# A layer's shift and scale: the products on GpSimd in place of TensorE's row products

## The chip, the cores and the metric

The kernel runs on one core of a Trainium2 chip. The metric is the device time of one launch in microseconds, the median of the runs. The profile is one further execution of the same program.

## The reference, cut to what matters

Two layers work on x of 256 tokens by 1024 channels, all in float32. Each layer is a token mixer (gated linear attention in the first, block attention, "MoBA", in the second) and an MLP. Ahead of each of these four parts x is normalised and then shifted and scaled by vectors that come from one conditioning vector c:

```python
c_act = jax.nn.silu(c)
for i in range(DEPTH):                       # 2
    mod = (c_act @ ada_w[i] + ada_b[i])      # ada_w[i]: 1024 x 6144
    sh1, sc1, g1, sh2, sc2, g2 = jnp.split(mod, 6, axis=-1)
    h = rms_norm(x, norm_mix_g[i]) * (1 + sc1) + sh1
    x = x + g1 * mixer(h)
    h = rms_norm(x, norm_mlp_g[i]) * (1 + sc2) + sh2
    x = x + g2 * (jnp.square(jax.nn.relu(h @ w1[i])) @ w2[i])
```

The product c_act @ ada_w is cut into 24 blocks of 512 columns, 12 a layer; a block's weights are 1024 x 512 numbers, 2 MB. Blocks 18 to 21 are the shift and scale (sh2, sc2) of the last MLP. They are what is changed.

## The kernel before, in words

Large products run on TensorE in three passes: ScalarE rounds a unit of weights to w_hi (line 860), VectorE subtracts to get w_lo (line 1186), and TensorE adds hi x hi, lo x hi and hi x lo (lines 428 to 430). Weights come from HBM by SyncE's queue into w_raw, eight units deep; w_hi and w_lo are rings of four units. A unit is 128 x 1024 numbers. Every engine's order is written out by hand, with semaphores between them.

A block of the second mixer's input projection (`moba`, six blocks n = 0 to 5) is four units. Behind a unit TensorE may do side work, held in `sides[n][u]`; ScalarE and VectorE have such lists under `tasks`, keyed by the block whose weights they prepare. From block 1 on each block is read out of PSUM, its heads' square sums are taken, it is rotated (`cosines`, `rotate`, `scale` on VectorE), and turned by TensorE (`turn_rot`, line 768).

The modulation blocks come in three ways. Most are loaded in two halves of 1 MB (512 of the 1024 rows of weights, as 128 partitions x 4 x 512) into the two halves of `ada_raw` by GpSimd's queue. VectorE multiplies the four slices of a half by their numbers of c_act and adds them into a slot of `ada_acc` (lines 1201 and 1204), and TensorE sums over the partitions: `fin_mods` (line 471) for shift and scale, sixteen products of a 128x128 piece with a column of ones, or `fin_gate` (line 503) for the gates. Blocks 0 to 3 and blocks 18 to 21 go to TensorE directly: `ada_rows` (line 488) makes four products for a half, each with one column of c_act as the stationary side, into partitions 0, 32, 64 and 96 of one bank; ScalarE copies the rows out (`ada_out`, line 900), and `ada_cols` (line 496) turns and sums them with a selector column in four small products. For blocks 18 to 21 the eight row groups stand behind units 1 and 2 of blocks 1 to 4 of `moba`, the selector groups behind unit 1 of blocks 2 to 5, and VectorE first clears the bank (`zero_rows`, line 1301). VectorE then adds the bias and makes the scale (`mods(3, 1)`), which TensorE waits for ahead of the attention's scores.

GpSimd's queue does nothing but start loads: each when the half of `ada_raw` that it overwrites has been used. Block 18 is loaded late in the first MLP; blocks 19 to 22 are each loaded when TensorE's row products have used the half before.

Of the kernel before, what the change touches and what calls it, by code (L numbers as in the profile page):

```python
# [28 lines left out]
ALU = mybir.AluOpType  # L29
ACT = mybir.ActivationFunctionType  # L30
X_AXIS = mybir.AxisListType.X

P = 128
TB = 2
COLS = 512
# [12 lines left out]
def trunk_kernel(nc, x_d, c_d, pos_d, ada_w, ada_b, mix_g, mlp_g, gla_in, gla_up, gla_bg, gla_og,  # L48
# [22 lines left out]
    mix_w = [(gla_in[0], gla_out[0]), (moba_in[0], moba_out[0])]  # L71


    ADA_PE = [[0, 2, 1, 3], [18, 19, 20, 21]]

    ctx = ExitStack()
    with ctx:
# [3 lines left out]
        def sem(name):  # L81
            return ctx.enter_context(nc.semaphore(name))
# [5 lines left out]
        ada_raw = sb("ada_raw", [P, 2, KC // 2, COLS])  # L88
        ada_acc = sb("ada_acc", [P, ADA_ACC, COLS])
# [9 lines left out]
        rows = sb("rows", [P, P])  # L99
        cols = sb("cols", [P, P])  # L100
        c_act = sb("c_act", [P, KC])
# [10 lines left out]
        K1 = 1024  # L112
# [3 lines left out]
        def area(at, *shape):  # L116

            n = 1
            for s in shape:
                n *= s  # L120
            assert at + n <= ARENA
            v = arena[:, at:at + n]
            if len(shape) == 2:
                v = v.rearrange("p (a b) -> p a b", a=shape[0])
            elif len(shape) == 3:
                v = v.rearrange("p (a b c) -> p a b c", a=shape[0], b=shape[1])
            return v
# [41 lines left out]

        ada_pre = [area((4 + 2 * i) * K1, KC // 2, COLS) for i in range(4)]  # L170

        ada_row = [area(13 * K1, 2, COLS)[0:97], area(10 * K1, 2, COLS)[0:97]]

        ps = ctx.enter_context(nc.psum_tensor("ps", [P, 8, COLS], F32))

# [13 lines left out]
        ada_mac = sem("ada_mac")  # L189
        set_up = sem("set_up")  # L190
        ada_sw_in = [sem(f"ada_sw_in{i}") for i in range(2)]
        ada_pre_in = [sem(f"ada_pre_in{i}") for i in range(4)]
        ada_pe = sem("ada_pe")
        row_ok = sem("row_ok")
        col_T = sem("col_T")
        c_in, c_T, c_ok = sem("c_in"), sem("c_T"), sem("c_ok")
        vec_T, vec_ok = sem("vec_T"), sem("vec_ok")
        mod_T, mod_red, mod_ok = sem("mod_T"), sem("mod_red"), sem("mod_ok")
        gate_p, gate_ok = sem("gate_p"), sem("gate_ok")
# [30 lines left out]

        ADA_FIRST = ADA_PE[0]
        SETS_SILU_SIN, SETS_LN_EXP = "silu_and_others", "natural_log_exp_and_others"

        def ada_turn(b):

            return b - 8 if isinstance(b, int) and b > ADA_PE[1][-1] else b - 4

# [7 lines left out]
        def acc_slot(b):  # L249
            return (b + 4) % ADA_ACC  # L250
# [25 lines left out]
        @block.gpsimd  # L276
        def _(pool):
            for half in range(2):
                pool.wait_ge(ada_pe, 6 + half + 1)
                nc.gpsimd.dma_start(ada_raw[:, half], ada_part(4, half)).then_inc(ada_sw_in[half], 16)  # L280

            def load(l, n, half):
                src = ada_w[l, half * 4 * P:(half + 1) * 4 * P, bass.ds(n * COLS, COLS)]
                nc.gpsimd.dma_start(ada_raw[:, half], src.rearrange("(k p) n -> p k n", p=P)  # L284
                                    ).then_inc(ada_sw_in[half], 16)


            for l, first, end in ((0, 5, 12), (1, 0, 7)):
                with pool.Fori(first, end) as n:
                    for half in range(2):  # L290
                        pool.wait_ge(ada_mac, 8 * n + 8 * ada_turn(12 * l - 1) + 4 * (half + 1))
                        load(l, n, half)
            with pool.Fori(7, 11) as n:
                for half in range(2):
                    pool.wait_ge(ada_pe, 2 * n - 2 * 7 + 8 + half + 1)
                    load(1, n, half)
            for half in range(2):
                pool.wait_ge(ada_mac, 8 * ada_turn(22) + 4 * (half + 1))
                load(1, 11, half)
# [124 lines left out]
        def _(pe):  # L424
# [40 lines left out]
            def fin_mods(v, bank):  # L465

                b0 = 12 * (v // 2) + 6 * (v % 2)
                pe.wait_ge(ada_mac, 8 * (ada_turn(b0 + 3) + 1))
                for i in range(4):
                    for q in range(4):  # L470
                        z = mm(ps[:, bank, 4 * i + q:4 * i + q + 1],
                               ada_acc[:, acc_slot(b0 + i), q * P:(q + 1) * P], ones[:, 0:1], start=True, stop=True)
                z.then_inc(mod_T, 1)

            def ada_rows(b, half, bank):


                if b in (0, 3):
                    raw = ada_raw[:, half]
                    pe.wait_ge(ada_in[half], 16 if b == 0 else 32)  # L480
                elif b < 4:
                    raw = ada_pre[2 * (2 - b) + half]
                    pe.wait_ge(ada_pre_in[2 * (2 - b) + half], 16)
                else:
                    raw = ada_raw[:, half]
                    pe.wait_ge(ada_sw_in[half], 16 * (b - 3))
                for k in range(4):
                    z = mm(ps[32 * k:32 * k + 1, bank, :], c_act[:, 4 * half + k:4 * half + k + 1], raw[:, k],  # L488
                           start=half == 0, stop=half == 1)
                z.then_inc(ada_pe, 1)  # L490

            def ada_cols(i, bank, c0=0):

                pe.wait_ge(row_ok, i + 1)
                for q in range(4):
                    z = mm(ps[:, bank, c0 + q:c0 + q + 1], ada_row[i // 4][:, i % 2, q * P:(q + 1) * P],  # L496
                           ones[0:97, 0:1], start=True, stop=True)
                z.then_inc(col_T, 1)

# [245 lines left out]
            def moba():  # L745
# [2 lines left out]
                    for i in range(2):  # L748
                        fin_gate(16 + i, 2 + i)

                def rows(i, half):

                    if i == 0:
                        pe.wait_ge(set_up, 3)
                    elif half == 0:
                        ada_cols(3 + i, 1, 4 * (i - 1))
                    ada_rows(18 + i, half, 0)

                def turn_rot(n):

                    pe.wait_ge(rot_ok, n + 1)
# [36 lines left out]
                        z.then_inc(oT_ok, 1)  # L798

                sides = [{}, {0: gate1}] + [{3: (lambda n=n: turn_rot(n))} for n in range(4)]  # L800
                for i in range(4):
                    for half in range(2):
                        sides[1 + i][1 + half] = lambda i=i, half=half: rows(i, half)
                sides[5][1] = lambda: ada_cols(7, 1, 12)
                for n in range(6):
                    if n >= 2:
                        pe.wait_ge(in_out, 12 + 2 * (n - 1))
# [36 lines left out]
        def _(act):  # L844
# [51 lines left out]
            def ada_out(i):  # L896
                act.wait_ge(ada_pe, 2 * i + 2)
                if i >= 2:
                    act.wait_ge(col_T, i - 1)
                A(ada_row[i // 4][:, i % 2], ps[0:97, 6 + i % 2 if i < 4 else 0, :], ACT.Copy).then_inc(row_ok, 1)  # L900

            def modulate_tile(v, tb, quarters):

# [119 lines left out]
            def moba():  # L1023
# [29 lines left out]
                def read_v(half):  # L1053
                    read_in(1, 4 + half, [b_v[:, tb, half * COLS:(half + 1) * COLS] for tb in range(TB)])

                tasks = {}
                for n in range(4):
                    tasks.setdefault((n + 2, 3), []).append(lambda n=n: ada_out(4 + n))
                    tasks.setdefault((n + 1, 3), []).append(lambda n=n: stats(n))
                    tasks.setdefault((n + 3 if n < 3 else 6, 3 if n == 3 else 0), []).append(lambda n=n: read_rot(n))  # L1060
                tasks[5, 3] = [lambda: read_v(0), lambda: ada_out(7)]
                tasks[(6, 3)] = [lambda: read_v(1), lambda: read_rot(3)]

                tasks[1, 0] = [sines]
# [108 lines left out]
        def _(dve):  # L1173
# [46 lines left out]
            def mods(v, bank):  # L1220

                l, s = v // 2, v % 2
                if v == 3:
                    dve.wait_ge(col_T, 8)
                else:
                    dve.wait_ge(mod_T, v)
                at = C_AB + (4 * l + 2 * s) * KC
                V.tensor_tensor(modc[:, l, 2 * s:2 * s + 2].rearrange("p a k -> p (a k)"), ps[:, bank, 0:2 * KC],
                                cols[:, at:at + 2 * KC], ALU.add).then_inc(mod_red, 1)
                dve.wait_ge(mod_red, 4 + v)  # L1230
                g = (C_MLP if s else C_MIX) + l * KC
                m = modc[:, l, 2 * s + 1]
                V.scalar_tensor_tensor(m, m, 1.0, cols[:, g:g + KC], op0=ALU.add, op1=ALU.mult
                                       ).then_inc(mod_ok, 1)
# [47 lines left out]
            def first_norm():  # L1282
# [11 lines left out]
                for i in range(2, 4):  # L1294
                    first_mods(i, ADA_FIRST[i], 4 + i)
                modulate(0, slice(0, SEQ), 0, 0, range(2, 4))

            def zero_rows():

                dve.wait_ge(a_ok, A_NORM[2] + 8)  # L1300
                V.memset(ps[:, 0, :], 0.0).then_inc(set_up, 1)

            def norm(v):

# [355 lines left out]
            for l in range(DEPTH):  # L1660
                if l == 0:
                    gla()
                else:
                    norm(2)
                    zero_rows()
                    moba()
                out_project(l)
                norm(2 * l + 1)
                mlp(l)
# [39 lines left out]
```

## Time and profile before

| | us |
|---|---|
| median of 3 runs | 687.27 |
| lowest and highest | 686.78, 690.5 |
| profiled execution, span from first to last instruction | 686.4 |
| TensorE busy | 646.6 |
| VectorE busy | 470.6 |
| ScalarE busy | 338.4 |
| GpSimd busy (starting DMAs) | 30.3 |

Of the profiled execution the page gives the span and no other time; the median is 0.9 us above it. The engines are called PE (TensorE; PEld its weight loads), DVE (VectorE), ACT (ScalarE), POOL (GpSimd) and SP (SyncE). L428 is line 428 of the kernel before. Matmuls are pipelined, so the spacing of their starts says more than their durations.

### The profile page before, as it was taken

The numbers are of one execution on the slowest core, as the hardware profiler recorded it, in microseconds if no ns is written. First come the engines' busy times: TensorE is split into PE (matmuls) and PEld (weight loads), VectorE is DVE, ScalarE is ACT, GpSimd is POOL, SyncE is SP. The second block draws the span as 40 slices with busy tenths as digits, with TensorE's granted clock in tenths as the row PEclk, the third lists the DMA queues.
The fourth block names the chain that finished last, engine by engine and source line by source line (L and its number), as shares of the span: only waits on it lengthen the run. The fifth ranks groups of instructions, "written<-read, shape, count | busy, mean of one in ns | idle before, by whom it ended". The sixth has DMA issues, their size and how long they took to land.

```text
span 686.4 us, 9712 instructions
## 1 busy us (share of the span) xinstructions
PE 646.6 (94%) x3594; PEld 535.0 (78%) x3594; DVE 470.6 (69%) x702; ACT 338.4 (49%) x562; POOL 30.3 (4%) x44
## 2 busy tenths in 40 slices
PE   4789999999999999999997999989999999999997
PEld 2457866677789988998885666667779998999885
DVE  2358999696787877787886846685678844555446
ACT  3244632544854345435427756665585445443440
POOL 0011010000000000000000000000000000000000
PEclk9889999999999999999999999999999999999999
DMA  8999778554598877878935677760349555565501
GB/s 305 380 377 352 244 265 309 198 176 154 181 317 311 296 250 270 317 258 287 343 118 183 221 270 246 259 230 1 123 145 336 193 185 187 184 182 198 195 32 61
DMA packets 61492, 156.87 MB, mean 229 GB/s; under 512 B 4124, under 2 KB 5000, under 8 KB 61464
## 3 DMA queue, kind: packets, MB, share of 16 engines
q1 hardware_dynamic: 50584, 114.56, 48.3%
q0 software_dynamic: 10880, 41.95, 17.5%
q8 instruction: 17, 0.28, 0.2%
q14 instruction: 11, 0.09, 0.0%
HBM read 155.44 MB, written 1.05 MB: 228 GB/s over the span
## 4 chain that ended last, share of the span: by engine, by line
PE 77%; DVE 12%; ACT 6%; DMA 2%; issue 2%; SPq 1%; ACTq 0%; DVEq 0%; POOLq 0%
PE ps L428 16%; PE ps L429 15%; PE ps L430 15%; PE ps L582 8%; PE ps L581 8%; PE ps L580 8%; DVE w_lo L1186 3%; ACT w_hi L860 2%; PE ps L488 2%; DVE ada_acc L1204 1%; DMA rows<-in_ada_b_dram 1%; DMA ada_raw<-in_ada_w_dram 1%; DVE a_lo L1329 1%; PE ps L512 1%; PE ps L496 1%
## 5 line engine op out<-in xcount | busy, mean ns | idle before, releaser
L1186 DVE TENSOR_TENSOR w_lo<-w_raw,w_hi 128x1024 fp32r<-128x1024 f32 x192 | 232.4, 1222 | 140.7 <-ACT w_hi L860 140.5
L860 ACT ACTIVATE w_hi<-w_raw 128x1024 fp32r<-128x1024 f32 x192 | 200.4, 1057 | 222.7 <-PE ps L430 116.8
L428 PE MATMUL ps<-w_hi,a_hi 128*128 128x512 f32 x288 | 121.1, 421 | 20.1 <-DVE a_lo L1329 14.1
L580 PE MATMUL ps<-a_hi,w_hi 128*128 128x256 f32 x448 | 126.9, 283 | 0.0
L582 PE MATMUL ps<-a_hi,w_lo 128*128 128x256 f32 x448 | 126.8, 283 | 0.0
L581 PE MATMUL ps<-a_lo,w_hi 128*128 128x256 f32 x448 | 126.8, 283 | 0.0
L429 PE MATMUL ps<-w_lo,a_hi 128*128 128x512 f32 x288 | 116.0, 403 | 0.0
L430 PE MATMUL ps<-w_hi,a_lo 128*128 128x512 f32 x288 | 115.5, 401 | 0.0
L428 PE MATMUL ps<-w_hi,m_hi 128*128 128x512 f32 x256 | 100.7, 393 | 0.0
L429 PE MATMUL ps<-w_lo,m_hi 128*128 128x512 f32 x256 | 100.4, 392 | 0.0
L430 PE MATMUL ps<-w_hi,m_lo 128*128 128x512 f32 x256 | 100.3, 392 | 0.0
L428 PEld LDWEIGHTS ps<-w_hi,a_hi 128*128 128x128 f32 x288 | 56.2, 195 | 47.2 <-issue 16.9
L1204 DVE SCALAR_TENSOR_TENSOR ada_acc<-ada_raw,c_act,ada_acc 128x512 f32<-128x512 f32 (+1 forms) x112 | 84.0, 750 | 3.5
L581 PEld LDWEIGHTS ps<-a_lo,w_hi 128*128 128x128 f32 x448 | 85.9, 192 | 0.6
L580 PEld LDWEIGHTS ps<-a_hi,w_hi 128*128 128x128 f32 x448 | 85.9, 192 | 0.5
L582 PEld LDWEIGHTS ps<-a_hi,w_lo 128*128 128x128 f32 x448 | 85.9, 192 | 0.0
L430 PEld LDWEIGHTS ps<-w_hi,a_lo 128*128 128x128 f32 x288 | 56.2, 195 | 12.5
L429 PEld LDWEIGHTS ps<-w_lo,a_hi 128*128 128x128 f32 x288 | 56.3, 196 | 10.6 <-issue 0.2
L428 PEld LDWEIGHTS ps<-w_hi,m_hi 128*128 128x128 f32 x256 | 48.5, 190 | 11.2 <-issue 1.4
L430 PEld LDWEIGHTS ps<-w_hi,m_lo 128*128 128x128 f32 x256 | 48.5, 189 | 10.2
L429 PEld LDWEIGHTS ps<-w_lo,m_hi 128*128 128x128 f32 x256 | 48.5, 189 | 9.6
L284 POOL DMA_DIRECT2D ada_raw<-in_ada_w_dram x38 | 28.5, 749 | 452.5 <-DVE ada_acc L1204 359.0
(158 smaller groups left out, 509.1 us busy)
## 6 DMA issues: line engine op xcount, KB each, us to landing
w_raw<-in_mlp_w_dram SPq DMA_DIRECT2D x64, 1024.0 KB, 5.4
ada_raw<-in_ada_w_dram POOLq DMA_DIRECT2D x40, 1024.0 KB, 6.0
w_raw<-in_gla_w_in_dram SPq DMA_DIRECT2D x12, 1024.0 KB, 11.1
w_raw<-in_moba_w_in_dram SPq DMA_DIRECT2D x12, 1024.0 KB, 6.3
ada_raw<-in_ada_w_dram SPq DMA_DIRECT2D x4, 1024.0 KB, 10.8
arena<-in_ada_w_dram SPq DMA_DIRECT2D x4, 1024.0 KB, 12.8
w_raw<-in_gla_w_out_dram SPq DMA_DIRECT2D x4, 1024.0 KB, 7.7
w_raw<-in_moba_w_out_dram SPq DMA_DIRECT2D x4, 1024.0 KB, 5.1
```

Source lines behind the costliest of these rows:

```text
L284: nc.gpsimd.dma_start(ada_raw[:, half], src.rearrange("(k p) n -> p k n", p=P)).then_inc(ada_sw_in[half], 16)
L428: mm(out, hi, w_hi[:, slot, wc], start=first, stop=False)
L429: mm(out, hi, w_lo[:, slot, wc], start=False, stop=False)
L430: return mm(out, lo, w_hi[:, slot, wc], start=False, stop=last)
L488: z = mm(ps[32 * k:32 * k + 1, bank, :], c_act[:, 4 * half + k:4 * half + k + 1], raw[:, k], start=half == 0, stop=half == 1)
L496: z = mm(ps[:, bank, c0 + q:c0 + q + 1], ada_row[i // 4][:, i % 2, q * P:(q + 1) * P], ones[0:97, 0:1], start=True, stop=True)
L580: mm(o, w_hi[:, u, w], a_hi[:, a, :], start=u == 0 and k == 0, stop=False)
L581: mm(o, w_hi[:, u, w], a_lo[:, a, :], start=False, stop=False)
L582: z = mm(o, w_lo[:, u, w], a_hi[:, a, :], start=False, stop=u == 3 and k == 1)
L860: A(w_hi[:, c % SPLIT], w_raw[:, c // 2, c % 2], ACT.Copy).then_inc(hi_made, 1)
L1186: V.tensor_tensor(w_lo[:, c % SPLIT], w_raw[:, c // 2, c % 2], w_hi[:, c % SPLIT].bitcast(F32), ALU.subtract).then_inc(lo_made, 1)
L1204: z = V.scalar_tensor_tensor(acc, w, s, acc, op0=ALU.mult, op1=ALU.add)
```

## The change

Blocks 18 to 21 are multiplied and summed by GpSimd, in place, in `ada_raw`: a half (128 x 2048 numbers) is multiplied by c_act, spread over the 512 columns; its four slices are then added to two, and these to one, which goes into a slot of `ada_acc` (the second half with one more sum). A wait on a semaphore stands between each two instructions. The first write into a slot waits until TensorE has read the block that the slot held before. After each half GpSimd starts the next load into it. TensorE's eight row groups and four selector groups for these blocks go, with VectorE's clearing of the bank and ScalarE's four copies; behind unit 1 of block 5 TensorE does `fin_mods(3, 1)`, which waits for GpSimd's last sum.

```diff
-            with pool.Fori(7, 11) as n:
+            pool.wait_ge(c_ok, 1)
+            for t, b in enumerate(ADA_POOL):          # 18, 19, 20, 21
+                acc = ada_acc[:, acc_slot(b)]
                 for half in range(2):
-                    pool.wait_ge(ada_pe, 2 * n - 2 * 7 + 8 + half + 1)
-                    load(1, n, half)
+                    i = 2 * t + half
+                    w = ada_raw[:, half]
+                    pool.wait_ge(ada_sw_in[half], 16 * (b - 3))
+                    nc.gpsimd.tensor_tensor(w, w, c_act[:, 4 * half:4 * half + 4, None].to_broadcast([P, 4, COLS]),
+                                            ALU.mult).then_inc(pool_mul, 1)
+                    pool.wait_ge(pool_mul, i + 1)
+                    nc.gpsimd.tensor_tensor(w[:, 0:2], w[:, 0:2], w[:, 2:4], ALU.add).then_inc(pool_sum, 1)
+                    pool.wait_ge(pool_sum, 3 * t + 1 + half)
+                    if i == 0:
+                        pool.wait_ge(gate_p, 4)
+                    elif i == 4:
+                        pool.wait_ge(mod_T, 2)
+                    if half == 0:
+                        nc.gpsimd.tensor_tensor(acc, w[:, 0], w[:, 1], ALU.add).then_inc(pool_ada, 1)
+                    else:
+                        nc.gpsimd.tensor_tensor(w[:, 0], w[:, 0], w[:, 1], ALU.add).then_inc(pool_sum, 1)
+                        pool.wait_ge(pool_sum, 3 * t + 3)
+                        pool.wait_ge(pool_ada, i)
+                        nc.gpsimd.tensor_tensor(acc, acc, w[:, 0], ALU.add).then_inc(pool_ada, 1)
+                    pool.wait_ge(pool_ada, i + 1)
+                    load(1, b + 1 - 12, half)
...
             def fin_mods(v, bank):
-                pe.wait_ge(ada_mac, 8 * (ada_turn(b0 + 3) + 1))
+                if v == 3:
+                    pe.wait_ge(pool_ada, 2 * len(ADA_POOL))
+                else:
+                    pe.wait_ge(ada_mac, 8 * (ada_turn(b0 + 3) + 1))
...
-                for i in range(4):
-                    for half in range(2):
-                        sides[1 + i][1 + half] = lambda i=i, half=half: rows(i, half)
-                sides[5][1] = lambda: ada_cols(7, 1, 12)
+                sides[5][1] = lambda: fin_mods(3, 1)
...
-                    tasks.setdefault((n + 2, 3), []).append(lambda n=n: ada_out(4 + n))
...
-                tasks[5, 3] = [lambda: read_v(0), lambda: ada_out(7)]
+                tasks[5, 3] = [lambda: read_v(0)]
...
-                    zero_rows()
```

## Rows read from the trace of the kernel before

**Rows 1.** The page: engines' busy time, and the chain's shares.
```profile
PE 646.6 (94%) x3594; PEld 535.0 (78%) x3594; DVE 470.6 (69%) x702; ACT 338.4 (49%) x562; POOL 30.3 (4%) x44
PE 77%; DVE 12%; ACT 6%; DMA 2%; issue 2%; SPq 1%; ACTq 0%; DVEq 0%; POOLq 0%
```

**Rows 2.** Timelines, 341 to 364 us: start, duration, engine, line, form [idle before].
```profile
341.29 1.88 PE L503 MATMUL ps<-ada_acc,ones 128*128 128x512 f32 x4
341.56 0.76 DVE L1560 CAST m_hi<-arena 128x512 fp32r<-128x512 f32 x2 [2.22 <-PE ps L430]
...
363.08 0.77 PE L428 MATMUL ps<-w_hi,a_hi 128*128 128x512 f32 x1 [2.79 <-DVE a_lo L1329]
```

**Rows 3.** Timeline of TensorE around the row and selector groups.
```profile
398.67 0.40 PE L430 MATMUL ps<-w_hi,a_lo 128*128 128x512 f32 x1
398.91 0.95 PE L496 MATMUL ps<-ones,arena 97*128 97x1 f32 x8
399.79 1.04 PE L488 MATMUL ps<-ada_raw,c_act 128*1 128x512 f32 x8
400.76 0.50 PE L428 MATMUL ps<-w_hi,a_hi 128*128 128x512 f32 x1
...
419.27 0.39 PE L430 MATMUL ps<-w_hi,a_lo 128*128 128x512 f32 x1
419.59 1.04 PE L488 MATMUL ps<-ada_raw,c_act 128*1 128x512 f32 x8
420.56 0.50 PE L428 MATMUL ps<-w_hi,a_hi 128*128 128x512 f32 x1
...
446.63 0.95 PE L496 MATMUL ps<-ones,arena 97*128 97x1 f32 x8
```

**Rows 4.** Timelines of TensorE and of VectorE, block 3.
```profile
411.94 0.50 PE L428 MATMUL ps<-w_hi,a_hi 128*128 128x512 f32 x1 [0.63 <-DVE w_lo L1186]
...
414.52 1.23 DVE L1186 TENSOR_TENSOR w_lo<-w_raw,w_hi 128x1024 fp32r<-128x1024 f32 x1
...
417.81 2.35 DVE L1186 TENSOR_TENSOR w_lo<-w_raw,w_hi 128x1024 fp32r<-128x1024 f32 x2
```

**Rows 5.** TensorE's timeline, and the stretch behind: busy by engine, PEclk, DMA share, GB/s.
```profile
348.37 0.39 PE L430 MATMUL ps<-w_hi,m_lo 128*128 128x512 f32 x1
348.60 3.62 PE L471 MATMUL ps<-ones,ada_acc 128*128 128x1 f32 x32
352.08 0.49 PE L428 MATMUL ps<-w_hi,m_hi 128*128 128x512 f32 x1
...
355.77 0.45 PE L428 MATMUL ps<-w_hi,m_hi 128*128 128x512 f32 x1
...
352.10:355.80 3.70, 3.70 (x12) 2.91 (x12) 3.57 (x7) 0.08 (x1) 0.00 (x0) 0.55 0.00 0
```

**Rows 6.** GpSimd's timeline and its loads' time to landing; a stretch with its DMA share.
```profile
332.43 0.75 POOL L284 DMA_DIRECT2D ada_raw<-in_ada_w_dram  x1 [6.63 <-DVE ada_acc L1204]
...
387.46 0.75 POOL L284 DMA_DIRECT2D ada_raw<-in_ada_w_dram  x1 [49.01 <-PE ps L488]
...
DMA to landing us min/median/max: 5.4/5.7/10.0
...
372.85:381.15 8.30, 8.30 (x37) 6.87 (x37) 3.17 (x6) 8.15 (x14) 0.00 (x0) 1.00 0.05 18
```

**Rows 7.** Groups by form, VectorE 338 to 448 us; ScalarE 381 to 454 us.
```profile
L1186 DVE TENSOR_TENSOR w_lo<-w_raw,w_hi 128x1024 fp32r<-128x1024 f32 x27 | 32.5, 1221 | 23.2 <-ACT w_hi L860 23.0
L1340 DVE TENSOR_TENSOR arena<-ps,gates 128x512 f32<-128x512 f32 x4 | 2.8, 688 | 0.0
L1259 DVE TENSOR_SCALAR arena<-x,stat 128x1024 f32<-128x1024 f32 x2 | 1.6, 814 | 0.1
...
L1038 ACT ACTIVATE arena<-arena 128x128 f32<-128x128 f32 x32 | 9.4, 296 | 0.3
```

**Rows 8.** Waits from 352 to 381 us: total, times, longest.
```profile
DVE a_lo L1329 <- ACT a_hi L915: 5.7, 4, 3.5
DVE stat L1255 <- ACT arena L873: 0.9, 1, 0.9
```

More of the change, by code:

```diff
@@ L71, in trunk_kernel @@
     mix_w = [(gla_in[0], gla_out[0]), (moba_in[0], moba_out[0])]
-    ADA_PE = [[0, 2, 1, 3], [18, 19, 20, 21]]
+    ADA_PE = [0, 2, 1, 3]
+    ADA_POOL = [18, 19, 20, 21]
     ctx = ExitStack()
@@ L170, in trunk_kernel @@
         ada_pre = [area((4 + 2 * i) * K1, KC // 2, COLS) for i in range(4)]
-        ada_row = [area(13 * K1, 2, COLS)[0:97], area(10 * K1, 2, COLS)[0:97]]
+        ada_row = area(13 * K1, 2, COLS)[0:97]
         ps = ctx.enter_context(nc.psum_tensor("ps", [P, 8, COLS], F32))
@@ L193, in trunk_kernel @@
         ada_pe = sem("ada_pe")
+        pool_mul, pool_sum, pool_ada = sem("pool_mul"), sem("pool_sum"), sem("pool_ada")
         row_ok = sem("row_ok")
@@ L229, in trunk_kernel @@
         N_VEC = 3 + 2 * DEPTH
-        ADA_FIRST = ADA_PE[0]
+        ADA_FIRST = ADA_PE
         SETS_SILU_SIN, SETS_LN_EXP = "silu_and_others", "natural_log_exp_and_others"
         def ada_turn(b):
-            return b - 8 if isinstance(b, int) and b > ADA_PE[1][-1] else b - 4
+            return b - 8 if isinstance(b, int) and b > ADA_POOL[-1] else b - 4
         N_PAIRS = [0, 4, 12, 20]
@@ L495, in ada_cols @@
                 for q in range(4):
-                    z = mm(ps[:, bank, c0 + q:c0 + q + 1], ada_row[i // 4][:, i % 2, q * P:(q + 1) * P],
+                    z = mm(ps[:, bank, c0 + q:c0 + q + 1], ada_row[:, i % 2, q * P:(q + 1) * P],
                            ones[0:97, 0:1], start=True, stop=True)
@@ L749, in gate1 @@
                         fin_gate(16 + i, 2 + i)
[L751 to L757, printed above, removed]
                 def turn_rot(n):
@@ L899, in ada_out @@
                     act.wait_ge(col_T, i - 1)
-                A(ada_row[i // 4][:, i % 2], ps[0:97, 6 + i % 2 if i < 4 else 0, :], ACT.Copy).then_inc(row_ok, 1)
+                A(ada_row[:, i % 2], ps[0:97, 6 + i % 2, :], ACT.Copy).then_inc(row_ok, 1)
             def modulate_tile(v, tb, quarters):
@@ L1222, in mods @@
                 l, s = v // 2, v % 2
[L1223 to L1226, printed above, removed]
+                dve.wait_ge(mod_T, v)
                 at = C_AB + (4 * l + 2 * s) * KC
@@ L1296, in first_norm @@
                 modulate(0, slice(0, SEQ), 0, 0, range(2, 4))
-            def zero_rows():
-                dve.wait_ge(a_ok, A_NORM[2] + 8)
-                V.memset(ps[:, 0, :], 0.0).then_inc(set_up, 1)
             def norm(v):
```

## The prediction

> **What bounds the kernel now.** I read the page first. TensorE is busy for 94% of the span and holds 77% of the chain that ended last; VectorE holds 12% of it [rows 1]. So work taken from TensorE is worth its own length only where TensorE is the link that is late, and work that slows VectorE costs where VectorE is. The change touches two stretches with different limits, which the chain of waits and the timelines separate.
>
> From 341.6 to 376.8 us (end of the first MLP, then the norm ahead of the second layer) the chain runs through VectorE: its link starts at 341.56 with m_hi, and TensorE's first matmul of the new layer at 363.08 has waited 2.79 us for VectorE's a_lo [rows 2].
>
> From 381 to 454 us (the second mixer's input projection) the chain is TensorE's matmuls with the rows' products between them. A projection unit is 12 matmuls, one every 0.23 us. From the last one before a selector and row group (398.67) to the first one behind it (400.76) are 2.09 us, and with a row group alone 419.27 to 420.56, 1.29 us [rows 3]. VectorE comes second here: TensorE waited 0.63 us for w_lo at 411.94 [rows 4].
>
> **Taken from TensorE.** A row group costs 1.29 - 0.23 = 1.06 us, eight of them 8.5 us. A selector group is 2.09 - 0.23 - 1.06 = 0.80 us, four of them 3.2 us. Together 11.7 us, all on the chain.
>
> **Put on TensorE.** fin_mods(3, 1), sixteen products of 128x128 with one column, takes the place of the last selector group (446.63 [rows 3]). The same form after the first MLP takes from 348.37 to 352.08, less one pitch: 3.5 us. Behind it the nine matmuls up to 355.77 take 3.69 us instead of 9 x 0.23 = 2.07, at a granted clock of 0.55, which is near the lower level of 1.2 GHz [rows 5]; before them TensorE did only one-column products. I expect the same dip: 1.6 us more. Sum 5.1 us; bounds 3.5 (no dip) and 5.1. Raw gain: 11.7 - 5.1 = 6.6 us.
>
> **What is late next.** In blocks 3 and 4, w_lo of a block's third unit starts at 414.52 and takes 1.22, so it is ready at 415.74, 3.80 us behind TensorE's start of the second unit at 411.94; without the rows TensorE is there after 12 x 0.23 plus about 0.1 = 2.86 us, so it waits 0.95 us. The fourth is ready at about 418.97 (the first of the two from 417.81 [rows 4], ended 1.15 later), 7.05 behind 411.94; TensorE comes at 3.80 + 2.86 = 6.7 and waits 0.35. Two blocks at 1.3 us take 2.6 us of the gain. In block 5 the 3.5 us of fin_mods cover this wait; in blocks 1 and 2 w_lo is further ahead. Remaining gain: 6.6 - 2.6 = 4.0 us. Bounds: 2.5 if block 2 loses as much, 6 without the clock dip.
>
> **Edits at nothing.** VectorE's clearing of a bank goes (one 128x512 instruction, not on the chain). ScalarE loses four copies of 97x512; it has idle time in these blocks, so no time comes back. The eight loads of blocks 19 to 22 no longer wait for TensorE (387.46 the first) but for GpSimd's own sums, and start from about 346 us on. POOL's queue holds nothing else before block 23, which VectorE takes up only in the second MLP. The DMA engines have room there: share 0.05 from 372.85 to 381.15 [rows 6]. If that cover were gone, w_raw would land later, and it has no slack worth naming in the blocks.
>
> **Put on GpSimd: its own time.** Per half a product over 2048 elements, a sum over 1024, a sum over 512, and per block one more of 512: 28 instructions, 30720 elements a partition. The trace has no arithmetic of GpSimd. Lower bound, VectorE's rows: 1.22 us for 1024 elements and 0.69 for 512 [rows 7], so 0.53 for 512 more and 2.28 for 2048; a block is 2 x 2.28 + 2 x 1.22 + 3 x 0.69 = 9.1 us, four are 36 us. Upper bound, far off: ScalarE's 0.296 us for 128 elements, 2.3 ns each [rows 7], 71 us. I take 36, since the row nearest in kind is VectorE's same instruction. The eight DMA instructions on POOL are 0.75 each, 6 us [rows 6].
>
> The Trainium skill's GPSIMD Engine Reference, "Performance versus the Vector engine", gives 4497 ns for a tensor_tensor of 2048 fp32. No run here shows it yet; the sum would then be about 68 us, an estimate.
>
> The first half is issued at 332.43 and lands 5.7 us later, 338.1 [rows 6]. TensorE wants the sums after the second unit of block 5, at 446.6 less the 8 us it gained till there, about 438. Between are 100 us. With 36 + 6 or 71 + 6 us GpSimd is early by itself: off the chain. The wait of TensorE on pool_ada has behind it all of TensorE, but it is met. The wait on gate_p is met with TensorE's gate products of 341.29, 1.88 us long [rows 2]; the one on mod_T with the products of 348 to 352.
>
> **Put on VectorE.** This term decides. w_lo, with two inputs in SBUF, takes 1.22 us for 1024 elements, while a one-input tensor_scalar of the same size takes 0.81 [rows 7]: VectorE has a second way into SBUF, which it uses either for a second input or for speed. If GpSimd's reads go that way too, the two engines exclude each other. Nothing in the trace shows it, since GpSimd computes nothing there. Bounds: 0, and the whole of GpSimd's time. A gain is excluded, as VectorE waits for nothing that GpSimd makes.
>
> With exclusion: GpSimd does 3.5 us of its work before 341.6 and holds back nothing. The other 36 - 3.5 = 32.5 us start beside VectorE's chain. That chain has over 40 instructions with two SBUF inputs or in the fast form, more than GpSimd's 26 left, so each of GpSimd's can fall between two of them. Hidden are VectorE's own waits up to 376.8, 5.7 + 0.9 us for ScalarE [rows 8], and its instructions that read PSUM and one SBUF tensor, six of 0.69 (four residual products, two gates; [rows 7] has the product), 4.1 us. Charged: 32.5 - 10.7 = 22 us. Once TensorE waits that long its clock falls as behind 2.79 us of idling (0.77 for the first matmul at 363.08 [rows 2] against 0.5 elsewhere); I add 2 us.
>
> SBUF — State Buffer, "Who interferes with whom", says it as a rule: a VectorE instruction with two SBUF inputs, or in a two-port mode, contends with a GpSimd instruction that reads SBUF, and whichever starts second is blocked for the other's full length. The trace agrees only in that two forms of one size differ, 0.81 against 1.22 us. By the rule with the skill's price above, the charge would be near 68 - 3.5 - 10.7 = 54 us, an estimate.
>
> **Sum, forecast (exclusion, GpSimd at VectorE's pace).** -4 + 22 + 2 = +20 us on the span of 686.4, 706.4. The median of the runs, 687.27, lies 0.9 us above that span, so 707. Its own range: 697 (half of GpSimd's time slips into waits) to 720.
>
> **Rivals.**
> 1. No contention, GpSimd off the chain. For it: no instruction of VectorE's w_lo is stretched beside POOL's DMA issues (mean 1221 ns over the window [rows 7]), though those are no reads of SBUF. Against it: the 0.81 against 1.22. Time: 687.3 - 4.0 = 683.3, from 681.3 to 685. This is the other side: faster. It decides if VectorE's instructions keep their lengths from 341 to 377 us.
> 2. Exclusion with GpSimd at its upper bound: 71 - 3.5 - 10.7 = 57 us charged, +2 - 4: 742; with longer instructions somewhat more falls into waits, so 725 to 742. It speaks for it that the engine is a different one and the only bound above is far; against it that instructions of 4 to 5 us would be needed.
> 3. Contention by shares: both engines go on, VectorE's port-using instructions stretched. From 341.6 to 376.8 they are about 23 us (35.2 less 10.7 and some issue time); half as long again adds 11, less 4: 694 to 700.
> 4. GpSimd late without contention: it decides from 94 us for 30720 elements, 3.1 ns each, above both bounds. At 4 ns it ends at 338 + 123 + 6 = 467, 29 us late: 712.
>
> **How the numbers follow.** Forecast 0.34, rival 1 0.29, rival 2 0.17, rival 3 0.16, rival 4 0.04. 0.5% is 3.4 us, about what a measurement here can tell from no change: faster means below 683.8. Rival 1 gives 0.17 below and 0.12 within; 0.03 of rival 3 falls within as well. Faster 0.17, same 0.15, slower 0.68. The range 682 to 736 leaves out about 0.06 below and 0.08 above.
>
> **What would show it.** Step by step: rows products gone from 381 to 454 us, blocks 3 and 4 at 14.3 us instead of 15.9 (411.94 to the same place in the next); sixteen one-column products there with a clock near 0.5 behind them; POOL busy about 40 us from 338 on; VectorE's small instructions of 345 to 352 us and w_lo and a_lo of 358 to 376 stretched or with gaps that nothing explains, and the new layer's first matmul at about 385 instead of 363. If that matmul stays at 363 the forecast is wrong and rival 1 holds; if POOL is busy 60 us or more and the matmul comes beyond 400, rival 2.

## The result, and the profile after

The changed kernel takes 740.06 us (739.37 to 740.45, four runs) against 687.67 for the kernel before: a ratio of 1.0746, 95% interval 1.0718 to 1.0773. The profiled execution has a span of 737.7 us, 51.3 more than before. I had forecast slower, 707 us, with a range to 736; the time lies beyond it, next to rival 2 (742).

Line numbers in the rows are each kernel's own. The page's shares. TensorE's busy time has not changed [rows 1]; VectorE's has grown by 54 us and its part of the chain from 12 to 21%:

```profile
PE 646.6 (88%) x3530; PEld 538.4 (73%) x3530; DVE 524.7 (71%) x701; ACT 336.4 (46%) x558; POOL 99.1 (13%) x72
PE 64%; DVE 21%; SPq 5%; ACT 4%; DMA 3%; issue 2%; DVEq 0%; ACTq 0%; POOLq 0%
```

GpSimd's groups from 330 to 430 us (busy, mean ns of one | idle before). The product over 2048 elements takes 3.61 us, where I had put 2.28. These 28 instructions are busy for 68.1 us; in their undisturbed lengths (3.61, 2.34, 1.26) they need 62.7:

```profile
L303 POOL TENSOR_TENSOR ada_raw<-ada_raw,c_act 128x2048 f32<-128x2048 f32 x8 | 28.9, 3610 | 1.4 <-DMA ada_raw<-in_ada_w_dram 1.2
L306 POOL TENSOR_TENSOR ada_raw<-ada_raw 128x1024 f32<-128x1024 f32 x8 | 20.5, 2567 | 0.6
L315 POOL TENSOR_TENSOR ada_raw<-ada_raw 128x512 f32<-128x512 f32 x4 | 7.1, 1785 | 0.3
L318 POOL TENSOR_TENSOR ada_acc<-ada_acc,ada_raw 128x512 f32<-128x512 f32 x4 | 6.0, 1499 | 0.3
L313 POOL TENSOR_TENSOR ada_acc<-ada_raw 128x512 f32<-128x512 f32 x4 | 5.6, 1402 | 0.3
```

The two engines side by side, timelines of 348 to 366 us. Read the ends: m_lo (0.68 us before the change) starts at 348.26 and ends at 353.07, 0.56 behind the end of GpSimd's product (348.90 + 3.61 = 352.51). A tensor_scalar of 0.29 us starts at 360.96, while GpSimd starts a load, and ends at 365.43, when the product behind that load has ended (361.65 + 3.61 = 365.26). Both had started before the product that held them, by the profile 0.64 and 0.69 us (the last section comes back to this):

```profile
348.26 4.81 DVE L1570 TENSOR_TENSOR m_lo<-arena,m_hi 128x512 fp32r<-128x512 f32 x1
348.90 3.61 POOL L303 TENSOR_TENSOR ada_raw<-ada_raw,c_act 128x2048 f32<-128x2048 f32 x1
...
360.83 0.80 POOL L286 DMA_DIRECT2D ada_raw<-in_ada_w_dram  x1 [1.11 <-issue]
360.96 4.47 DVE L1639 TENSOR_SCALAR arena<-arena 128x256 f32<-128x256 f32 x1
361.65 3.61 POOL L303 TENSOR_TENSOR ada_raw<-ada_raw,c_act 128x2048 f32<-128x2048 f32 x1
```

VectorE's groups, held and not held: one of the kernel before (338 to 448 us), then the changed kernel's from 330 to 500. The forms with two SBUF inputs grow from 0.43 to 1.93 us (L1634 before, L1641 now) and from 0.69 to 2.11 (L1348); the one that reads PSUM stays at 0.68, where it had 0.69 [rows 7]:

```profile
L1634 DVE SCALAR_TENSOR_TENSOR arena<-arena 128x256 f32<-128x256 f32 x6 | 2.5, 425 | 0.2
...
L1641 DVE SCALAR_TENSOR_TENSOR arena<-arena 128x256 f32<-128x256 f32 x6 | 11.6, 1934 | 0.2
L1348 DVE TENSOR_TENSOR x<-x,arena 128x512 f32<-128x512 f32 x4 | 8.4, 2109 | 0.1
L1347 DVE TENSOR_TENSOR arena<-ps,gates 128x512 f32<-128x512 f32 x4 | 2.7, 681 | 0.0
```

And where it lands: TensorE's first matmul of the second layer, 363.08 before [rows 2], and behind it the blocks (the second unit of blocks 3 and 4, 462.62 and 477.05, is 14.43 us apart; before, 411.94 [rows 4] and 427.83, the row that stands first here, 15.89). Last, the clock behind the sixteen products of fin_mods(3), which start at 494.33:

```profile
427.83 0.50 PE L428 MATMUL ps<-w_hi,a_hi 128*128 128x512 f32 x1 [0.63 <-DVE w_lo L1186]
...
413.22 0.77 PE L452 MATMUL ps<-w_hi,a_hi 128*128 128x512 f32 x1 [11.98 <-DVE a_lo L1336]
...
462.62 0.50 PE L452 MATMUL ps<-w_hi,a_hi 128*128 128x512 f32 x1 [0.63 <-DVE w_lo L1201]
466.48 0.50 PE L452 MATMUL ps<-w_hi,a_hi 128*128 128x512 f32 x1 [0.85 <-DVE w_lo L1201]
...
477.05 0.50 PE L452 MATMUL ps<-w_hi,a_hi 128*128 128x512 f32 x1 [0.63 <-DVE w_lo L1201]
...
494.33 3.79 PE L498 MATMUL ps<-ones,ada_acc 128*128 128x1 f32 x32
...
498.00:500.70 2.70, 2.70 (x8) 2.12 (x9) 2.70 (x3) 0.00 (x0) 0.00 (x0) 0.50 0.36 51
```

VectorE's w_lo that stands behind the norm starts at 432.97 where it started at 376.80. Less 0.6 us that this execution was late already at 333 us, 55.6 us are lost between. From there to the end 4.9 us come back: 56.2 less 51.3.

Not all of the 55.6 is VectorE. The last twelve matmuls ahead of the norm's transposes start 54.47 us later than before (367.37, now 421.84, behind a wait for VectorE's a_lo), the transposes behind them 56.21 us later (370.39, now 426.60): the twelve took 3.02 us and now take 4.76, at a granted clock of 0.57, near the lower level. TensorE had waited 11.98, 1.81 and 1.01 us ahead of its three groups of matmuls from 413.22 on. So 53.9 us come from VectorE and 1.7 from TensorE's clock; the rows are two of before, two of now, and the stretch (windows, as [rows 5]):

```profile
367.37 0.47 PE L428 MATMUL ps<-w_hi,a_hi 128*128 128x512 f32 x1
370.39 1.03 PE L512 MATMUL ps<-eye,arena 128*128 128x128 f32 x8
...
421.84 0.76 PE L452 MATMUL ps<-w_hi,a_hi 128*128 128x512 f32 x1 [1.01 <-DVE a_lo L1336]
426.60 1.03 PE L539 MATMUL ps<-eye,arena 128*128 128x128 f32 x8
421.84:426.60 4.76, 4.76 (x13) 3.71 (x14) 1.32 (x2) 0.00 (x0) 0.00 (x0) 0.57 0.90 315
```

### The profile page after: what moved, and what is told of

Its sections match the earlier page's. It is cut to its first block, busy times and chain, and to the rows that moved or that the text cites. A ratio compares the mean times of both kernels' runs of the same rounds, so it can differ in the third digit from the quotient of the medians.

```text
span 737.7 us, 9577 instructions
## 1 busy us (share of the span) xinstructions
PE 646.6 (88%) x3530; PEld 538.4 (73%) x3530; DVE 524.7 (71%) x701; ACT 336.4 (46%) x558; POOL 99.1 (13%) x72
## 4 chain that ended last, share of the span: by engine, by line
PE 64%; DVE 21%; SPq 5%; ACT 4%; DMA 3%; issue 2%; DVEq 0%; ACTq 0%; POOLq 0%
PE ps L452 13%; PE ps L454 12%; PE ps L453 12%; PE ps L608 7%; PE ps L609 7%; PE ps L607 7%; DVE w_lo L1201 6%; DVE ada_acc L1219 2%; DMA w_raw<-in_gla_w_in_dram 2%; DVE arena L1641 2%; ACT w_hi L876 1%; DVE x L1348 1%; DVE a_lo L1336 1%; PE ps L498 1%; DMA ada_raw<-in_ada_w_dram 1%
## 5 line engine op out<-in xcount | busy, mean ns | idle before, releaser
L1201 DVE TENSOR_TENSOR w_lo<-w_raw,w_hi 128x1024 fp32r<-128x1024 f32 x192 | 242.7, 1276 | 138.2 <-ACT w_hi L876 138.0
L452 PE MATMUL ps<-w_hi,m_hi 128*128 128x512 f32 x256 | 102.6, 401 | 7.6 <-DVE m_lo L1570 4.7
```

The lines of the kernel that those rows point to most:

```text
L452: mm(out, hi, w_hi[:, slot, wc], start=first, stop=False)
L1201: V.tensor_tensor(w_lo[:, c % SPLIT], w_raw[:, c // 2, c % 2], w_hi[:, c % SPLIT].bitcast(F32), ALU.subtract).then_inc(lo_made, 1)
```

## The experiments

Theory: a GpSimd instruction that reads SBUF and a VectorE instruction that uses the second way exclude each other for their whole length, and GpSimd's time is laid into VectorE's chain. Rivals: sharing; a cost of the waits, loads or one-column products; a cost that comes only from the place.

**p1_ports: each pair of forms by itself.** A separate kernel, no diff.

```python
for f in dve_forms: for g in pool_forms:   # VectorE: six of f, one by one; GpSimd: one of g
```

> A kernel by itself, which computes nothing of the reference: in each of 20 stretches VectorE runs six instructions of one form, one at a time (two SBUF inputs; one SBUF input; PSUM and SBUF input; PSUM input; a write alone; 512 elements each), while GpSimd runs one instruction (tensor_tensor over 2048, tensor_scalar over 2048, memset over 2048, or the start of a DMA). Exclusion: the two-input form (0.69 us alone) and the one-input fast form (0.42 alone) that overlap GpSimd's tensor_tensor last until its end, 3 to 4 us, once; those that read PSUM and the write alone keep their length. Sharing: the first two forms are stretched by at most 2 and all the while. Beside GpSimd's memset only the one-input fast form is held, if the write side is another path.

VectorE's timeline, six instructions a row; in each form the rows stand beside GpSimd's tensor_tensor, tensor_scalar, memset and DMA start, in this order (of L27 the first). L25 has two SBUF inputs, L26 one, L27 PSUM and SBUF:

```profile
10.92 8.50 DVE L25 TENSOR_TENSOR c<-a,b 128x512 f32<-128x512 f32 x6 [8.98 <-DMA h<-in_x_dram]
19.58 7.64 DVE L25 TENSOR_TENSOR c<-a,b 128x512 f32<-128x512 f32 x6
27.39 4.33 DVE L25 TENSOR_TENSOR c<-a,b 128x512 f32<-128x512 f32 x6
31.88 4.33 DVE L25 TENSOR_TENSOR c<-a,b 128x512 f32<-128x512 f32 x6
...
38.27 6.91 DVE L26 TENSOR_SCALAR c<-a 128x512 f32<-128x512 f32 x6
45.33 7.78 DVE L26 TENSOR_SCALAR c<-a 128x512 f32<-128x512 f32 x6
53.27 4.41 DVE L26 TENSOR_SCALAR c<-a 128x512 f32<-128x512 f32 x6
57.85 2.81 DVE L26 TENSOR_SCALAR c<-a 128x512 f32<-128x512 f32 x6
...
64.13 4.32 DVE L27 TENSOR_TENSOR c<-ps,b 128x512 f32<-128x512 f32 x6
```

GpSimd's timeline, its four forms where nothing disturbs them (beside L27):

```profile
64.18 4.51 POOL L32 TENSOR_TENSOR g<-g,h 128x2048 f32<-128x2048 f32 x1 [0.28 <-DVE c L78]
68.98 5.37 POOL L33 TENSOR_SCALAR g<-g 128x2048 f32<-128x2048 f32 x1 [0.29 <-DVE c L78]
74.60 1.80 POOL L34 MEMSET g<- 128x2048 f32 x1 [0.26 <-DVE c L78]
79.31 0.81 POOL L57 DMA_DIRECT2D land<-in_ada_w_dram  x1 [2.91 <-DVE c L78]
```

Two inputs in SBUF: 4.33 becomes 8.50 beside GpSimd's tensor_tensor of 4.5, so nearly its whole length is added, and 4.33 stays beside a memset. One input, the fast form: 2.81 becomes 6.91, and 4.41 beside the memset of 1.80, so writes hold it too. What reads PSUM, and VectorE's own memset (0.48 each in all four), are never held. Exclusion is shown, sharing is out: in each held row one instruction takes the whole delay and the others keep their lengths. GpSimd is held too: its tensor_tensor takes 4.99 us where VectorE's first instruction had begun 0.05 us ahead of it.

One pair falls short of "whole length". Beside GpSimd's tensor_scalar the two-input form gains only 3.3 us (7.64): its second instruction ends at 24.32, and a third runs from 24.36 while GpSimd's is recorded until 25.50. The one-input form is held by the same tensor_scalar to its end (7.78, 5.0 more). Why is not shown. GpSimd's one-input tensor_scalar (5.37) is slower than its tensor_tensor.

**e1_no_arith: the rest of the change alone.**

```diff
-  nc.gpsimd.tensor_tensor(w, w, c_act[...].to_broadcast([P, 4, COLS]), ALU.mult)
+  nc.gpsimd.tensor_tensor(w[:, :, 0:2], w[:, :, 0:2], c_act[...].to_broadcast([P, 4, 2]), ALU.mult)   # and so the sums
```

> The changed kernel with each of GpSimd's 28 instructions cut to 2 columns; the rest of its arithmetic is left out. All else stays: waits, loads, TensorE's sixteen products in place of the rows. Theory (exclusion of GpSimd's and VectorE's instructions): the whole loss goes, first matmul of the second layer back at about 363 us, and what is left is TensorE's saving less VectorE's lateness, 682 to 684 us, ratio 0.992 to 0.995. Rival (the loss lies in the waits, the loads or the one-column products): at or above 690.

683.84 us, ratio 0.9933 (0.9904 to 0.9962). The new layer's first matmul is back at 363.64. So the whole loss is GpSimd's arithmetic, and the edits on TensorE are worth about what the sum had without it, 683.3.

**e4_writes: GpSimd only writes.**

```diff
-  nc.gpsimd.tensor_tensor(w, w, ...)      # and the sums
+  nc.gpsimd.memset(w, 0.0)                # the same outputs
```

> The changed kernel with GpSimd's 28 instructions turned into memsets of the same outputs: GpSimd reads nothing, and the arithmetic of these four blocks is left out. If only GpSimd's reads shut out VectorE's two-input forms: w_lo and a_lo keep 1.22 and 0.42 us, while casts and tensor_scalar over SBUF are still held; 684 to 700 us. If any GpSimd instruction excludes them: the loss is the memsets' whole time, some 30 us or more, 710 to 735.

691.75 us, ratio 1.0052 (1.0030 to 1.0073). VectorE's timeline: the two-input forms keep their lengths (three of L1640 in 1.34), the tensor_scalars are held (1.96 for two of 0.25):

```profile
344.36 2.35 DVE L1200 TENSOR_TENSOR w_lo<-w_raw,w_hi 128x1024 fp32r<-128x1024 f32 x2
346.83 1.96 DVE L1627 TENSOR_SCALAR arena<-arena,stat 128x64 f32<-128x64 f32 x2
...
351.11 1.34 DVE L1640 SCALAR_TENSOR_TENSOR arena<-arena 128x256 f32<-128x256 f32 x3
352.49 2.21 DVE L1643 TENSOR_SCALAR arena<-arena 128x128 f32<-128x128 f32 x1
```

The first matmul comes at 370.89, 7.3 us behind the run without arithmetic. The two-input forms are free of GpSimd's writes, then. What share of the 56 us needs GpSimd's reads is not measured by this run: its memsets are busy for 29 us, less than half of the 62.7.

**e2_after_norm: the place.**

```diff
-            pool.wait_ge(c_ok, 1)
+            pool.wait_ge(a_ok, A_NORM[2] + 8)
```

> The changed kernel, but GpSimd's arithmetic begins only after VectorE's last a_lo of the norm ahead of the second layer (about 377 us). Exclusion: from 341 to 377 us as before the change; then GpSimd needs 63 us of its own, some 8 of DMA starts and gaps and 20 to 30 of VectorE's instructions between, so it ends at 468 to 478, 30 to 40 us after TensorE wants the sums in block 5 (438): 713 to 725 us. Rival (the charge is GpSimd's time wherever it lies): 740 again. Rival (no wait for the sums, VectorE's slack in the blocks hides the most): below 705.

736.36 us, ratio 1.0695 (1.0656 to 1.0735): a miss of my 713 to 725. The nearest of the three cases written down is the rival by which GpSimd's time is charged wherever it lies (740). I had reckoned with TensorE waiting for the sums. It never does: GpSimd ends at 461.7, and TensorE waits for w_lo instead. The stretch 378 to 462 us (busy of PE, PEld, DVE, ACT, POOL) and TensorE's waits from 376 to 500:

```profile
378.00:462.00 84.00, 43.80 (x143) 32.01 (x141) 83.20 (x49) 28.37 (x78) 78.58 (x36) 0.74 0.44 150
PE ps L452 <- DVE w_lo L1201: 43.9, 11, 9.2
```

VectorE, with idle time in these blocks before, is 83.2 of 84 us occupied, mostly held. Its slack there hides only 4 us more than the norm does.

**e6_half: half the arithmetic** (blocks 20 and 21 cut to 2 columns).

```diff
+                    n = COLS if t < 2 else 2
```

> The changed kernel with the arithmetic of blocks 20 and 21 cut to 2 columns, the rest of it left out; blocks 18 and 19 in full. If the loss is GpSimd's time, instruction by instruction, half of the 56 us goes: 683.8 + 26 to 30 = 710 to 714. If it comes from a few places at the start of the work (the casts and angles) that the first two blocks already cover, 725 to 740.

714.3 us, ratio 1.0354 (1.0319 to 1.0388). From 683.8 to 740.1 are 56.3 us; half the work costs 30.5, a little over half and 0.3 us above my 710 to 714. The cost goes with GpSimd's time.

**e5_pieces: shorter instructions.**

```diff
-  nc.gpsimd.tensor_tensor(w, w, ... [P, 4, COLS], ALU.mult)
+  for k in range(4):                       # no wait between them
+      nc.gpsimd.tensor_tensor(w[:, k], w[:, k], ... [P, COLS], ALU.mult)
```

> The changed kernel with GpSimd's products over 2048 elements cut into four of 512 and its sums over 1024 into two of 512: 60 instructions in place of 28, none over about 1.3 us, some 69 us of its own time in place of 63. Theory (strict turns: each VectorE instruction that needs the shared way waits for at most one of GpSimd's): from 341 to 377 us of the old clock VectorE has a bit over 40 such instructions, each now held by at most 1.2 us; 45 to 50 us are charged there and the rest falls into the blocks, where part hides: 725 to 737. Rival (GpSimd's whole time is charged wherever it runs): 744 to 750. Rival (short instructions slip between VectorE's): below 715.

737.97 us, ratio 1.0686 (1.0651 to 1.0722), just above my 725 to 737 and below the rival's 744. The strict turns that I had assumed came in one place and not in the other. The sums are in turn: of two with no wait between them, m_lo waits for the first (343.48 + 1.32 = 344.80), ends 0.55 us behind it (345.35), and the second takes 1.71 in place of 1.26. The four products are not: they run off in 4.02 us, and the w_lo that started at 349.16 ends only behind all of them (354.38). The timelines:

```profile
343.48 1.32 POOL L308 TENSOR_TENSOR ada_raw<-ada_raw 128x512 f32<-128x512 f32 x1
343.60 1.75 DVE L1572 TENSOR_TENSOR m_lo<-arena,m_hi 128x512 fp32r<-128x512 f32 x1
344.76 1.71 POOL L308 TENSOR_TENSOR ada_raw<-ada_raw 128x512 f32<-128x512 f32 x1
...
346.95 7.43 DVE L1203 TENSOR_TENSOR w_lo<-w_raw,w_hi 128x1024 fp32r<-128x1024 f32 x2
348.45 0.79 POOL L286 DMA_DIRECT2D ada_raw<-in_ada_w_dram  x1 [0.30 <-POOL ada_acc L315]
349.26 4.02 POOL L304 TENSOR_TENSOR ada_raw<-ada_raw,c_act 128x512 f32<-128x512 f32 x4
```

Of the eight groups of four products, seven stand directly behind the start of a load, and in each an instruction of VectorE that began beside that start was held until the fourth product ended. In the first group, which waited for its data instead, a cast of VectorE got its turn between the third product and the fourth (341.54 to 342.50). So it is not the missing wait that keeps VectorE out; what does, behind a load's start, stays open.

**e7_parts_no_arith: fin_mods(3) spread over four blocks**, GpSimd's arithmetic left out as in e1.

```diff
-                sides[5][1] = lambda: fin_mods(3, 1)
+                for i in range(4):
+                    sides[2 + i][1] = lambda i=i: fin_mods(3, 1, [i])
```

> As the run without GpSimd's arithmetic (683.8, the arithmetic left out), but TensorE's sixteen one-column products of fin_mods(3) in four groups of four, behind the second unit of blocks 2 to 5. Theory (TensorE's clock falls behind 3.5 us of one-column products and costs 1.3 us; in blocks 3 to 5 VectorE is 0.85 us late there anyway and hides the groups): 3 us less than with the sixteen together, ratio to before 0.988 to 0.990. Rival (the dip costs nothing since VectorE is the bound in block 5): 0.992 to 0.994.

681.42 us, ratio 0.9864 (0.9837 to 0.9892), against 0.9933 with the sixteen together: the direction is shown, and the medians give a size as expected or more. In the two profiled executions the blocks (VectorE's w_lo from the 101st to the 125th) take 93.63 us in place of 95.35, 1.7 less, so the trace bears out a little over half of the 3 us.

**e8_before_parts: the same for fin_mods(1) and (2), in the kernel before.**

```diff
-  out_project(l, {0: lambda: turn_o(1), 3: lambda: fin_mods(1, 4)})
+  out_project(l, {0: lambda: turn_o(1), 1: lambda: fin_mods(1, 4, [0, 1]), 2: ..., 3: ...})
```

> The kernel before, row products and all, with fin_mods(1) and fin_mods(2), which stand in both kernels, in parts: two groups of four products behind unit 1 and one behind units 2 and 3 of the first output projection, and one behind each unit of the first half of the first MLP's last step. If the clock's fall behind them is on the chain: 1.6 us less for the first, 0 to 1 for the second, 684.5 to 687 against 687.7 to 689, ratio 0.996 to 0.998. If not: 1.000.

688.63 us, ratio 0.9991 (0.9972 to 1.0010): nothing that can be told from no change, and a gain at the small end of what I had written down (0.998) is not excluded. The clock's fall is gone from the same stretches (windows, as [rows 5]; 0.52 and 0.55 before). The third row is the first stretch in e9 (below), which leaves fin_mods(1) as it was:

```profile
154.60:158.00 3.40, 3.40 (x17) 2.79 (x17) 2.88 (x6) 0.42 (x1) 0.00 (x0) 1.00 1.00 382
352.10:355.80 3.70, 3.70 (x18) 3.05 (x17) 2.49 (x7) 1.45 (x4) 0.00 (x0) 1.00 0.00 1
154.60:158.00 3.40, 3.40 (x17) 2.81 (x17) 3.29 (x7) 0.00 (x0) 0.00 (x0) 1.00 0.98 372
```

So the same sixteen products are not followed by a fall in every execution. And the fall does cost in the first place: without it VectorE's 33rd w_lo comes 12.2 us behind its 31st (e8) or 12.1 (e9), with it 13.7 (before), and the 1.4 us stay until 358 us. In e8's execution 1.0 us of it went again from 458 to 461 us, where TensorE's products of the attention run at the lower clock this time. A profiled execution is thus good for a microsecond or so either way, and only the medians over many runs compare kernels here.

**e9_read_later: the wait behind the transposes, in the kernel before.**

```diff
-  tasks.setdefault((n + 3 if n < 3 else 6, 3 if n == 3 else 0), []).append(lambda n=n: read_rot(n))
+  tasks.setdefault((n + 3 if n < 3 else 6, 3 if n == 3 else 2), []).append(lambda n=n: read_rot(n))
```

> The kernel before, with ScalarE's copy of the turned heads (read_rot) behind its third w_hi of a block instead of its first, so that w_hi and w_lo of the second and third unit no longer wait for TensorE's transposes. If that wait is what makes TensorE stand 0.63 us at the second unit of blocks 3 to 5, and VectorE's lateness with it: 2 to 3 us less, ratio 0.9955 to 0.998. Rival (the transposes of the next block or the fourth w_hi are then late by as much): 0.999 to 1.001.

685.69 us, ratio 0.9957 (0.9938 to 0.9977): faster than both kernels, by about what was expected. In its profiled execution the blocks (101st to 125th w_lo) take 96.6 us in place of 100.2. TensorE's idle time for w_lo is gone from these blocks; ScalarE's wait for the transposes, 21.3 us in the kernel before, is 11.0:

```profile
ACT arena L1049 <- PE ps L768: 11.0, 3, 3.7
```

**e10_read_later_no_arith: that edit on top of e7**, GpSimd's arithmetic left out.

```diff
+  tasks.setdefault((n + 3 if n < 3 else 6, 3 if n == 3 else 2), []).append(lambda n=n: read_rot(n))
```

> The run with fin_mods(3) in four parts and no arithmetic on GpSimd (left out), with the same later read_rot. If VectorE's lateness behind the transposes is what ate 2.6 us of TensorE's saving in blocks 3 and 4: 2 to 4 us less than 681.4, ratio to before 0.981 to 0.985. Rival (VectorE's rotation itself is the bound): 0.986 again.

676.96 us, ratio 0.9826 (0.9802 to 0.9850), against 0.9864 (0.9837 to 0.9892) without the edit. These intervals touch; the traces are clearer, with 88.7 us for the same blocks in place of e7's 93.6. The gains add: most of VectorE's lateness in the blocks came from ScalarE's place in line, not from its own rotation.

## Why the prediction was wrong, point by point

- **Taken from TensorE, put on it, and late next: right.** I had -4.0 us; from 432.97 on 4.9 came back, and e1 as a whole is worth 0.67%, 4.6 us. The waits in a block are 0.63, 0.85 and 0.28 us, where I had 0.95 and 0.35 beside the 0.63 that stays, and a block takes 14.43, where I had 14.3. The clock fell to 0.50 for 2.7 us behind fin_mods(3), in which six matmuls started in place of twelve, 1.3 us lost; I had 3.7 us and 1.6 lost. That it falls there at all was partly luck: behind fin_mods(1) it fell in one execution and not in another (e8, e9).
- **Exclusion as the mechanism: right**, and now shown form by form (p1, e4), as is the step that one instruction of GpSimd falls between two of VectorE's (m_lo ends 0.56 us behind the product, and then w_lo has its turn).
- **GpSimd's own time: the step that failed.** "I take 36, since the row nearest in kind is VectorE's same instruction." It is 62.7 us. A row of another engine is no measure of GpSimd; here it gave 0.57 of the truth. The far bound, ScalarE's 71, was nearer. The plain product of 2048 took 4.51 us in p1, the one with c_act spread out 3.61. The estimate from the Trainium skill's GPSIMD Engine Reference, "Performance versus the Vector engine", 68 us, was the nearest, and p1 agrees with the 4.497 us of that section.
- **What is hidden: too much.** I took off 3.5 us of work done before 341.6 and 10.7 us of VectorE's own waits and PSUM reads. The data landed later than I had it, so GpSimd began at 340.32 and had done 1.9 us when VectorE wanted its first cast at 342.18. Of the other 60.8 us 53.9 were charged, so 6.9 were hidden and not 10.7. The longest waits that I had counted, 5.7 us for ScalarE's a_hi, hid nothing: VectorE came to them at 423 us and later, when GpSimd had ended (418.9). With 62.7 in the place of 36 my own sum would have been 62.7 - 14.2 = 48.5 charged and 734, inside the range; this second error, 5.4 us, is what took it beyond.
- **The 2 us for TensorE's clock: about right.** The twelve matmuls from 421.84 to 426.60, on the chain, took 1.7 us more than before.
- **GpSimd early enough, off the chain: right.** Its last sum ended at 418.9; TensorE began fin_mods(3) at 494.3 with no wait.
- **Rival 2 is what came:** exclusion with a GpSimd nearly as slow as the far bound (62.7 of 71). I gave it 0.17 and held against it that it needs instructions of 4 to 5 us; the longest took 3.61, and the sum came all the same. My range ended at 736, below its 742.
- **The Trainium skill's rule** (SBUF — State Buffer, "Who interferes with whom") holds in the forms tried: two SBUF inputs against GpSimd's reads and not against its writes, the two-port form against both, PSUM readers never. The full length does not hold in one pair of p1: two SBUF inputs beside GpSimd's tensor_scalar. By the rule and the Trainium skill's price the charge was 54 us, an estimate, and 53.9 came. So near a hit was luck: the 68 was 5 us too long, and the 14.2 taken off as hidden 5 us too much.

## What to carry to other kernels

Before moving elementwise work to an idle GpSimd, look at what VectorE runs in those microseconds: each of its instructions with two SBUF inputs, or in the fast one-input form over SBUF, stands still while a GpSimd tensor_tensor runs, so the moved work is added to VectorE's chain at GpSimd's slower pace (here 63 us of GpSimd's work, 56 us lost, against 4.6 us saved on TensorE). Of the forms tried, those that read PSUM and a memset go on beside it. And ask of a wait of some tenths of a microsecond, repeated in every block, who stands in front in the queue: moving one copy two places on gave 0.4%.

## What the runs showed of the hardware that I had not expected

- GpSimd's tensor_scalar over 2048 elements takes 5.37 us, longer than its tensor_tensor with two full inputs (4.51) and with a broadcast input (3.61); its memset takes 1.80.
- A product directly behind a load's start holds VectorE from before its own recorded start. In the changed kernel six instructions of VectorE began beside such a start, 0.35 to 0.69 us before the product (m_lo at 348.26, the tensor_scalar at 360.96), and each was held until the product had ended; one that began with the load's start, 0.81 us before, got through (369.47). A load's start alone does not do it: in p1 six tensor_scalars beside one kept their 2.81 us, and in e1, where nothing follows the start for over a microsecond, a w_lo begun 0.27 us into it keeps its 1.22. Whether the product really begins earlier than the profile says stays open.

```profile
359.02 0.79 POOL L286 DMA_DIRECT2D ada_raw<-in_ada_w_dram  x1 [0.30 <-POOL ada_acc L319]
359.29 1.22 DVE L1202 TENSOR_TENSOR w_lo<-w_raw,w_hi 128x1024 fp32r<-128x1024 f32 x1
```

- Four products with no wait between them, directly behind a load's start, keep VectorE out as one; two sums with no wait between them let it in (e5).
- GpSimd waits as well: its sums over 1024 elements, 2.34 us alone, took up to 3.21 in the changed kernel, when a w_lo was in front of them.
- Behind the same sixteen one-column products, fin_mods(1), the granted clock was 0.52 in one execution and 1.00 in another (before, e9).
